# A twelfth place for one weight tile in each expert stage, and norm rows laid over the partitions by TensorE

## The reference

```python
def first_block(x, ...):
    for i in range(DEPTH):                       # 2: mlstm, then gla
        h = mixer(x, ...)
        x = layer_norm(ALPHA * x + h, ln_g[i, 0], ln_b[i, 0])
        y = ec_moe(x, moe_router[i], moe_w_gate[i], moe_w_up[i], moe_w_down[i])
        x = layer_norm(ALPHA * x + y, ln_g[i, 1], ln_b[i, 1])
    return x

def ec_moe(x, w_router, w_gate, w_up, w_down):   # 16 experts, 32 tokens each
    aff = softmax(x @ w_router)
    gates, idx = top_k(swapaxes(aff, 1, 2), 32)
    xin = x[idx]
    h = silu(xin @ w_gate) * (xin @ w_up)        # per expert, 1024 x 1024 each
    out = (h @ w_down) * gates
    return zeros_like(x).at[idx].add(out)
```

## Time and profile before

| | |
|---|---|
| median of 3 runs (range) | 1592.81 us (1592.26 to 1593.27) |
| the profiled execution | 1592.34 us, its span 1590.5 us |
| TensorE busy | 1309.8 us (82%) |
| VectorE, ScalarE, GpSimd busy | 303.6, 215.1, 88.5 us |
| moved by DMA | 501.34 MB, mean 315 GB/s |
| mean granted TensorE clock | 0.935 |

### The profile page before, as it was taken

How to read it: one execution, slowest core, us unless ns; L and a number is a source line. 1 busy time by engine, 2 the same in 40 slices (tenths; PEclk the granted TensorE clock), 3 DMA queues, 4 the chain that set the end, 5 groups by cost and what they waited for, 6 DMA issues and landing times.

```text
span 1590.5 us, 19235 instructions
## 1 busy us (share of the span) xinstructions
PE 1309.8 (82%) x8543; PEld 733.8 (46%) x8543; DVE 303.6 (19%) x747; ACT 215.1 (14%) x446; POOL 88.5 (6%) x106
## 2 busy tenths in 40 slices
PE   9999978568667679999886667667679999999998
PEld 7454533223223235655533223223235854988843
DVE  1153301001001002554310000001003032222201
ACT  1132100000000001441200000000001033211100
POOL 0001000000000001450000000000001022000000
PEclk9999998888888899999998988988889999999999
DMA  9917799999999999625799999999999941443000
GB/s 346 391 68 301 316 427 428 427 428 427 427 427 427 427 414 371 246 112 222 290 427 427 428 427 428 427 427 427 428 420 382 352 155 53 159 150 141 0 0 27
DMA packets 88258, 501.34 MB, mean 315 GB/s; under 512 B 8348, under 2 KB 31248, under 8 KB 63856
## 3 DMA queue, kind: packets, MB, share of 16 engines
q1 hardware_dynamic: 85152, 490.23, 75.9%
q0 software_dynamic: 3024, 9.89, 1.8%
HBM read 499.02 MB, written 1.07 MB: 314 GB/s over the span
## 4 chain that ended last, share of the span: by engine, by line
PE 52%; DMA 39%; DVE 4%; another core or an unknown queue 2%; ACT 1%; issue 1%; SPq 0%; POOL 0%; DVEq 0%; ACTq 0%
DMA phase_room<-in_moe_w_down 15%; PE bank L1172 10%; DMA weight_ring<-in_moe_w_down 9%; DMA weight_ring<-in_moe_w_gate 6%; PE bank L725 6%; DMA weight_ring<-in_moe_w_up 6%; PE bank L771 5%; PE bank L1028 5%; PE bank L1206 5%; PE bank L742 5%; PE bank L1080 3%; PE bank L1067 3%; PE bank L730 3%; DMA phase_room<-in_moe_w_gate 2%; PE bank L950 1%
## 5 line engine op out<-in xcount | busy, mean ns | idle before, releaser
L1028 PE MATMUL bank<-weight_ring,x_tok 128*32 128x256 f32 x3328 | 229.0, 424 | 123.9 <-DMA weight_ring<-in_moe_w_up 104.8
L1028 PEld LDWEIGHTS bank<-weight_ring,x_tok 128*32 128x32 f32 x3328 | 112.0, 119 | 235.7 <-issue 98.2
L1067 PE MATMUL bank<-weight_ring,xT 128*32 128x512 f32 x864 | 132.2, 745 | 85.9 <-DMA weight_ring<-in_moe_w_down 79.4
L1172 PE MATMUL bank<-xT,weight_ring 128*128 128x256 f32 (+1 forms) x768 | 153.1, 362 | 0.3 <-ACT xT L1237 0.3
L1172 PEld LDWEIGHTS bank<-xT,weight_ring 128*128 128x128 f32 x768 | 136.3, 191 | 16.8 <-issue 0.6
L1080 PE MATMUL bank<-x_tok,xT 128*128 128x512 f32 x256 | 124.5, 631 | 0.0
L1875 DVE TENSOR_TENSOR xT<-xT,bank 128x256 f32<-128x256 f32 x32 | 13.5, 421 | 477.2 <-PE bank L1028 477.2
L1067 PEld LDWEIGHTS bank<-weight_ring,xT 128*32 128x32 f32 x864 | 28.0, 122 | 164.0 <-issue 71.0
L725 PE MATMUL bank<-xT,weight_ring 128*128 128x256 f32 x448 | 97.6, 380 | 0.7 <-ACT phase_room L1268 0.7
L725 PEld LDWEIGHTS bank<-xT,weight_ring 128*128 128x128 f32 x448 | 85.2, 191 | 13.6 <-ACT phase_room L1268 1.5
L1080 PEld LDWEIGHTS bank<-x_tok,xT 128*128 128x128 f32 x256 | 49.2, 203 | 86.8 <-issue 86.8
(11 more groups left out here) (241 smaller groups left out, 1047.1 us busy)
## 6 DMA issues: line engine op xcount, KB each, us to landing
weight_ring<-in_moe_w_up SPq DMA_DIRECT2D x54, 2048.0 KB, 50.1
weight_ring<-in_moe_w_down SPq DMA_DIRECT2D x54, 2048.0 KB, 49.4
weight_ring<-in_moe_w_gate SPq DMA_DIRECT2D x50, 2048.0 KB, 49.5
phase_room<-in_moe_w_gate SPq DMA_DIRECT2D x14, 2048.0 KB, 49.0
weight_ring<-in_w_up SPq DMA_DIRECT2D x22, 1024.0 KB, 7.7
phase_room<-in_moe_w_up SPq DMA_DIRECT2D x10, 2048.0 KB, 49.9
phase_room<-in_moe_w_down SPq DMA_DIRECT2D x8, 2048.0 KB, 49.7
weight_ring<-in_gla_w_in SPq DMA_DIRECT2D x6, 2048.0 KB, 22.3
```

Source lines behind the costliest of these rows:

```text
L1028: last = mm(bank[q * CAP:(q + 1) * CAP, 0:S], xinT[:, 4 * r + k, j * CAP:(j + 1) * CAP], w[:, k, q * S:(q + 1) * S], start=(r == 0 and k = ...
L1067: last = mm(PS[i][k * CAP:(k + 1) * CAP, :], hidT[:, 4 * r + k, :], w[:, k, i * 512:(i + 1) * 512], start=(r == 0), stop=(r == 1), skip_gr ...
L1172: last = mm(PS[bank_pair + c // 2][:, at + tokens.start:at + tokens.stop], w[:, k, c * P:(c + 1) * P], xT[:, k, tokens], start=(k == 0), s ...
```

## The change

Tile 19 in layer 0 and tile 123 in layer 1, the last down tile of expert 1, get a place of their own, used once. It is made of `norm_rows` (two of its four rows of 1024), `head_gain` and the first half of `xT`. SP waits for `logits_part` and loads it in three DMAs. All tiles behind take their places in the ring one later.

Since the region is now in use until expert 1 is through, three things move. The selection of group 0 goes to `affT_t`; the slot numbers are kept in `small`, and groups 1 to 3 are selected at the end of expert 2, into the second to fourth quarter of that half of `xT`. The norm's gain and bias (and in layer 1 the attention gain) come as 8 blocks of 128 numbers each, into `phase_room`; TensorE multiplies them with a column of the identity that picks one block and is repeated 128 times, four blocks into one bank per round, in experts 8 to 11 (layer 0) or 8 to 13 (layer 1), and ScalarE copies the bank to its half row. The broadcast of the GLA gain goes behind the small GLA loads.

```diff
+T_ONCE = [base + SLOTS + ROOM_SLOTS for base in T_MOE]
+ONCE = SLOTS + ROOM_SLOTS
 def ring_plan():
...
+        if n in T_ONCE:
+            slots.append(ONCE)
+            before.append(None)
+            continue
...
+    norm_blocks = room[0:24, 1056:1056 + P]
+    spread_rows = [x[:, 512 * i:512 * (i + 1)] for x in (gain_row, bias_row, ng_t) for i in range(2)]
+    ROUNDS, FIRST_ROUND = (4, 6), 8
+    sels = [x.rearrange("p (t n) -> p t n", t=TT)
+            for x in [affT_t] + [sel_t[:, 256 * g:256 * (g + 1)] for g in range(1, NG)]]
+    token_slots = small[:, 96:96 + TT * E]
+    once_rows = [gb_t[:, 0:D], gb_t[:, D:2 * D], ng_t[:, :], xT_t[:, 0:D]]
...
         def experts(layer):
...
+                if n in T_ONCE:
+                    sp.wait_ge(logits_part, layer + 1)
+                    sp.dma_start(gb_t[:, :], src[:, 0:2 * D]).then_inc(once_landed, 16)
+                    for k in (2, 3):
+                        sp.dma_start(once_rows[k], src[:, k * D:(k + 1) * D]).then_inc(once_landed, 16)
+                elif i < E * TPE - 1:
                     load(n, src)
...
         def moe_small(layer, u_moe):
...
-            norm_rows(t["ln_g"][layer, 1], t["ln_b"][layer, 1])
+            rows = [t["ln_g"][layer, 1], t["ln_b"][layer, 1], t["attn_norm_2"][0]]
+            for i in range(ROUNDS[layer] // 2):
+                pool.dma_start(norm_blocks[8 * i:8 * i + 8], rows[i].rearrange("(n p) -> n p", p=P)
+                               ).then_inc(blocks_landed, 16)
...
-        row(ng_t[:, :], t["gla_norm_g"][0], gain_landed)
...
         pool.dma_start(gate_b_rows, t["gla_gate_b"][0].rearrange("d (n p) -> (d n) p", p=P)
                        ).then_inc(small_landed[3], 16)
+        row(ng_t[:, :], t["gla_norm_g"][0], gain_landed)
         pool.wait_ge(b_ready, 1)
...
-        row(attn_row, t["attn_norm_2"][0], gain_landed)
...
             for e in range(E):
...
                 def tile(c):
-                    arrived(pe, base + TPE * e + c)
+                    if base + TPE * e + c in T_ONCE:
+                        pe.wait_ge(once_landed, 48 * (layer + 1))
+                    else:
+                        arrived(pe, base + TPE * e + c)
...
                 if j == 0:
+                    if g == 1:
+                        pe.wait_ge(sel_ready, 2 * layer + 2)
                     gather(g, 0)
...
                 pe.wait_ge(hid_done, n + 1)
+                if 0 < e - FIRST_ROUND <= ROUNDS[layer]:
+                    pe.wait_ge(rows_written, sum(ROUNDS[:layer]) + e - FIRST_ROUND)
                 for r in range(2):
                     up_products(2, r, PS[3])
...
                 pe.wait_ge(hid_done, n + 2)
+                if 0 <= e - FIRST_ROUND < ROUNDS[layer]:
+                    blocks = 4 * ROUNDS[layer]
+                    pe.wait_ge(blocks_landed, 8 * sum(ROUNDS[:layer + 1]))
+                    for i in range(4):
+                        pick = 4 * (e - FIRST_ROUND) + i
+                        last = mm(PS[3][:, i * P:(i + 1) * P], ident[0:blocks, pick:pick + 1].to_broadcast([blocks, P]),
+                                  norm_blocks[0:blocks], start=True, stop=True)
+                    last.then_inc(blocks_spread, 1)
...
                 f(selT, PS[2][:, S:2 * S], ACT.Copy).then_inc(turned_copied, 1)
+                if 0 <= e - FIRST_ROUND < ROUNDS[layer]:
+                    act.wait_ge(blocks_spread, sum(ROUNDS[:layer]) + e - FIRST_ROUND + 1)
+                    f(spread_rows[e - FIRST_ROUND], PS[3][:, :], ACT.Copy).then_inc(rows_written, 1)
                 act.wait_ge(half_out, n + 1)
...
-            for e0, e1 in ((0, EG), (EG, E)):
+            def select(g, of):
...
+            select(0, PS[3]).then_inc(sel_ready, 1)
+            link(v.tensor_copy(token_slots, PS[3][:, 0:TT * E]))
...
                 v.tensor_copy(exp_t[:, 512:1024], PS[1][:, :]).then_inc(exp_dve, 1)
+                if e == EG - 2:
+                    dve.wait_ge(tile_used, T_ONCE[layer] + 1)
+                    for later in range(1, NG):
+                        last = select(later, token_slots)
+                    last.then_inc(sel_ready, 1)
```

More of the change, by code:

```diff
@@ L230, in build_in @@
     sel_t, turned_t = xT_t[:, 0:1024], xT_t[:, 1024:1024 + 2 * S]
+    sels = [x.rearrange("p (t n) -> p t n", t=TT)
+            for x in [affT_t] + [sel_t[:, 256 * g:256 * (g + 1)] for g in range(1, NG)]]
+    token_slots = small[:, 96:96 + TT * E]
+    once_rows = [gb_t[:, 0:D], gb_t[:, D:2 * D], ng_t[:, :], xT_t[:, 0:D]]
     hid, silu_g = xT_t[:, 1536:1536 + S], xT_t[:, 1792:1792 + S]
     xinT = xin_t.rearrange("p (k n) -> p k n", k=KC)
-    sel = sel_t.rearrange("p (t n) -> p t n", t=TT)
     selg = selg_t.rearrange("p (t n) -> p t n", t=TT)
@@ L278, in build_in @@
     landed = [sem(f"landed{i}") for i in range(SLOTS + ROOM_SLOTS)]
+    once_landed = sem("once_landed")
+    blocks_landed, blocks_spread, rows_written = sem("blocks_landed"), sem("blocks_spread"), sem("rows_written")
     tile_used = sem("tile_used")
@@ L381, in slot, with tile_rows @@
         return room[:, at:at + TILE]
+    def tile_rows(n):
+        if n in T_ONCE:
+            return once_rows
+        return [slot(n)[:, k * D:(k + 1) * D] for k in range(4)]
     def landings(n):
@@ L483, in experts @@
                 n, src = T_MOE[layer] + i, ws[c // 2][e, c % 2]
-                if i < E * TPE - 1:
+                if n in T_ONCE:
+                    sp.wait_ge(logits_part, layer + 1)
[3 more added lines that the diff above has]
+                elif i < E * TPE - 1:
                     load(n, src)
@@ L1006, in gather @@
                         last = mm(PS[quarter % 2][:, at:at + P], x_perm[:, tt, k, :],
-                                  sel[:, tt, g * P:(g + 1) * P], start=(tt == 0), stop=(tt == TT - 1))
+                                  sels[g][:, tt], start=(tt == 0), stop=(tt == TT - 1))
                 last.then_inc(xin_done, 1)
@@ L1014, in tile @@
                 def tile(c):
-                    arrived(pe, base + TPE * e + c)
-                    return slot(base + TPE * e + c).rearrange("p (k n) -> p k n", k=4)
+                    if base + TPE * e + c in T_ONCE:
+                        pe.wait_ge(once_landed, 48 * (layer + 1))
+                    else:
+                        arrived(pe, base + TPE * e + c)
+                    return tile_rows(base + TPE * e + c)
                 def up_products(c, r, bank):
@@ L1029, in up_products @@
                                       xinT[:, 4 * r + k, j * CAP:(j + 1) * CAP],
-                                      w[:, k, q * S:(q + 1) * S],
+                                      w[k][:, q * S:(q + 1) * S],
                                       start=(r == 0 and k == 0), stop=(r == 1 and k == 3),
@@ L1059, in moe @@
                         pe.wait_ge(last_columns_landed, 16 * (layer + 1))
-                        w = slot(base + TPE * e + 5).rearrange("p (k n) -> p k n", k=4)
+                        w = tile_rows(base + TPE * e + 5)
                     else:
@@ L1067, in moe @@
                             last = mm(PS[i][k * CAP:(k + 1) * CAP, :], hidT[:, 4 * r + k, :],
-                                      w[:, k, i * 512:(i + 1) * 512],
+                                      w[k][:, i * 512:(i + 1) * 512],
                                       start=(r == 0), stop=(r == 1), skip_group_check=True)
@@ L1598, in layer_norm @@
             if tt == 0:
-                dve.wait_ge(rows_landed, 32 * (use + 1))
+                if use % 2 == 0:
+                    dve.wait_ge(rows_landed, 32 * (use // 2 + 1))
+                else:
+                    dve.wait_ge(rows_written, sum(ROUNDS[:use // 2]) + 4)
             for j in range(2):
@@ L1819, in rms @@
             if tt == 0:
-                dve.wait_ge(*((gain_landed, 48), (rows_landed, 32 * 4 + 16), (gain_landed, 64))[u])
+                dve.wait_ge(*((rows_written, sum(ROUNDS)), (rows_landed, 32 * 2 + 16), (gain_landed, 48))[u])
             v.scalar_tensor_tensor(acc[:, tt], x_tok[:, tt], inv_spread[:, n:n + 1], gain,
@@ L1847, in moe @@
             dve.wait_ge(slotsT_done, layer + 1)
-            for e0, e1 in ((0, EG), (EG, E)):
+            def select(g, of):
                 for tt in range(TT):
                     last = v.tensor_tensor(
-                        sel[:, tt, e0 * CAP:e1 * CAP].rearrange("p (e c) -> p e c", c=CAP),
-                        slot_ids.unsqueeze(1).to_broadcast([P, e1 - e0, CAP]),
-                        PS[3][:, tt * E + e0:tt * E + e1].unsqueeze(2).to_broadcast([P, e1 - e0, CAP]),
+                        sels[g][:, tt].rearrange("p (e c) -> p e c", c=CAP),
+                        slot_ids.unsqueeze(1).to_broadcast([P, EG, CAP]),
+                        of[:, tt * E + g * EG:tt * E + (g + 1) * EG].unsqueeze(2).to_broadcast([P, EG, CAP]),
                         ALU.is_equal)
-                last.then_inc(sel_ready, 1)
-            dve.wait_ge(sel_ready, 2 * layer + 2)
```

(10 more changed lines are left out.)

## The result

The changed kernel takes 1580.57 us, the median of four executions (1580.15 to 1580.84), against 1592.61 before (1592.26 to 1593.27): 0.9924 of the time, interval 0.9906 to 0.9941. That is 12.0 us less. Over all sixteen executions of the changed kernel the median is 1581.3 and the gain 11.3 us.

What follows compares the result with a forecast made beforehand. The weight stream was taken to bound both expert stages. One tile less in each, -4.9 us twice, made -9.8 us with all other terms 0: 1582.5 us, plus 0.5 to the median, 1583.0 us; range 1580.8 to 1588.0.

Steps and rivals of the forecast that it cites:

- the free stretch: Some 8 us ahead of each weight stream, such as 162 to 170 us, with the DMA engines 2% busy or less.
- the beat: Time of one tile in the weight stream, read from each stage's last expert: 4.9 us.
- one tile, once, in each stage: In both expert stages, one tile fewer follows the first release: -4.9 us each, -9.8 us in all.
- distance is worth nothing more: In the ring, with some ten tiles queued once the stream runs, a twelfth place adds no further gain.
- followed by 84 tiles where 85 had followed: At the first release tile 20 goes out, with one tile fewer behind it in the stream than before.
- what the start or the tail may gain or lose: Allowance of 1.5 us in the likeliest case's own range of 1581 to 1585 us.
- The costs set to nothing: Broadcasts, rounds on TensorE, ScalarE copies, VectorE selections and SP's order: each put at 0, hidden in waits or free time.
- The cover: TensorE's waits for weights ahead of tile 4, 6.3 us per expert, hide the rounds, which would otherwise cost 10 to 21 us.
- The pieces: Tile 19's three DMAs of 1024, 512 and 512 KB overlap, ending near 164; one after another, 174.1, or 167.5 by the skill.
- Given back at the GLA stage: Rival, 0.04: GLA weights, issued one use later, come late by a tile; the first stage's gain is lost, 1587.9 us.
- The pieces don't fit: Rival, 0.04: the three DMAs go one after another, end at 174.1, and 1.1 us of each gain is left, 1590.6 us.
- Slower, by the clock: Rival, 0.03: at 1.2 GHz for whole experts TensorE sets the pace and the rounds add 21 us, 1604 us.

Runs made afterwards that it cites:

- the kernel with the late tile: The changed kernel, but the twelfth tile's three DMAs wait until tile 8 is used instead of for the logits: 1589.23 us, ratio 0.998.
- both repeats: The changed kernel, unchanged, measured twice more over six executions each: 1582.08 us and 1581.17 us.
- the kernel in which the last one lands at 174.1: The changed kernel, but the twelfth tile waits for VectorE's slot numbers instead of the logits: 1582.61 us, ratio 0.9935.

## Where the prediction was right, and which step of it failed

**The mechanism was right.** The forecast was one tile less in each unbroken stream, because it flows in the free stretch. With everything but the place there is no gain (1592.48); with the place in one stage half of it (1587.5); with both all of it. In 162 to 170 us the tile's traffic ends at 163.3, the release stays 4.0 us behind the first gather (169.19 - 165.21, before 169.97 - 165.99), and the beat in the last expert is 4.89 us as before.

**The step that failed is the size of the term "one tile, once, in each stage", -9.8 us,** and with it the step by which nothing was added to it, "distance is worth nothing more". In the two profiles that were compared first the stages are 5.6 and 5.1 us shorter, 10.7 together. Over two profiles of the kernel before and three of the changed one they are 429.48 and 429.75 against 424.04 and 424.67 us: 5.4 and 5.1, together 10.5. The 4.9 us were read from the last expert alone. In all stages of all profiles, the 81 tiles from the third behind the release to the last whole one land 4.94 to 4.95 us apart in the mean, some of them 6 us behind the one before. And the start of the stream, which the sum does not have at all, was a little less thin: in the 12 us behind the release the kernel before has 350 and 359 GB/s in the first stage of its two profiles, the changed one 371, 365 and 369; in the second stage it is 343 and 365 against 366, 355 and 365. That is some 0.4 and 0.2 us of stream. 4.95 + 0.4 and 4.95 + 0.2 come near to 5.4 and 5.1. But these rates overlap between the kernels (the changed kernel with its rounds four times over has 356 and 363), so a less thin start is not shown to belong to the change; it may be chance.

**"Distance is worth nothing more" was wrong**, by 0.8 and 0.9 us a stage in the kernel with the late tile. The argument looked at the ten tiles that are queued once the stream runs, and not at the first us, in which a single one is. Whether the changed kernel has a share of this gain is not shown. (In the same place the prediction lets tile 20 be "followed by 84 tiles where 85 had followed"; these counts include the first tile. The difference, one, is right.)

**From the forecast to the first median.** The forecast was 2.4 us too high. 0.9 of it are the stages. 0.8 were gained ahead of the first gather and 0.2 behind the second stage, and 0.5 are the step from the profiled execution to the median, added because the median of the first three executions lay that far above the profiled one; in the changed kernel the two agree (1580.58 and 1580.57). All but the 0.9 I take for the luck of a few executions.

**The range was too tight below.** Its low end missed the first median by 0.2 us and held both repeats. It allowed 0.5 us for the beat and 1.5 for "what the start or the tail may gain or lose", and ended at 1580.8. Over all sixteen executions 0.8 us of the 11.3 are not in the stages. In the means of the profiles, 0.5 us are gained ahead of the first gather and 0.4 behind the second stage, and 0.6 lost between the stages. I can assign these to no part of the change; single segments vary by more (164.8 to 169.5 us ahead of the gather over the eleven profiles). The range was made from the forecast's terms and had too little for the chance in a median of few executions, where single ones of one kernel lie 5 to 7 us apart.

**The costs set to nothing were nothing.** Broadcasts, blocks, rounds, copies, selections: 1592.48 against 1592.64 without the place. Ten rounds measured 13.4 us, 1.3 each where 1.0 to 2.1 were estimated; they are free even four times over. The cover was read too small: the 203.2 us of waits, 6.3 an expert, leave out the tiles in the phase room, with which they are 237.3, 7.4 an expert. They shrank by 36 us where 20 to 25 were forecast.

**The pieces.** They overlap, as I took it: 1024, 512 and 512 KB are in 163.3 - 156.0 = 7.3 us after the first issue, where one DMA of 2048 KB took 7.2. The Trainium skill (SBUF — State Buffer, The DMA setup-cost knee) puts about 2 us on each transfer besides its bytes, and calls them mostly the latency of its completion. The 10.8 us of the prediction, an estimate from these figures, add them up three times, which the page does not say of transfers in flight together; one transfer of 2048 KB is 2 + 4.8 = 6.8 us by the page, an estimate too. The trace agrees with one such latency for all three, at least for transfers issued within 0.9 us. It would not have mattered: with the last piece at 174.1 the time was the same.

**The rivals.**

- *Given back at the GLA stage*: fell. Both marks, the last products and the first of the GLA stage, moved by the same 6.38 us, and the stretch between the stages is 173.75 us where it was 173.74.
- *The pieces don't fit*: fell. They fit. And the kernel in which the last one lands at 174.1 loses nothing; there it is a late issue and not pieces in turn that makes it late, so a transfer in turn was not measured.
- *Slower, by the clock*: fell. In 171 to 588 us the mean granted clock is 0.88 and the beat in the last expert 4.89 us, as before, and the waits for tiles left in the changed kernel, 201 us, cover three more sets of rounds.

## What to carry to other kernels

Where a stage is bound by a stream of weights, look at the stretch ahead of it for time in which the DMA engines rest because all places are taken. Here one more place that can be filled there took one beat and a little off the stage, once, and the work to make room for it was free, since it fell into waits for the stream. I expect the same of a further place as long as the stretch has time for its bytes, and did not measure one. The tile had to be asked for one beat before the stream starts, and did not have to arrive by then. And before a range ends 2 us beyond the forecast, look at how far single executions of one kernel lie apart.

## What the runs showed that I had not expected

- The start of a stream is thin when one tile is queued: 284 to 421 GB/s from the sixth to the ninth us behind the release in the profiles that I read, against 456 to 459 when two tiles go out together. Over the first 12 us that is 343 to 371 GB/s against 371, so it costs 0 to 0.8 us of stream, differing from execution to execution, and is made up nowhere behind. The kernel with two queued had stages shorter by 0.8 and 0.9 us; half of it is seen there, and the other half has no shown cause.
- An unchanged kernel moves from 1590.3 to 1597.2 us. Two places of such differences are seen in profiles, both with the granted clock: ahead of the first gather (twelve records in 5.31 or 6.55 us) and at the first products of the GLA stage (5.42 or 7.11 us), in code that is the same in all of these kernels.
